# Seventy-five more products on cleared operands at the head of TensorE's program

## The reference

```python
x = x + 0.5 * post1(SwiGLU_1(pre1(x)))
u = pre_mix(x);  [MLA inputs | MoBA q,k,v] = u @ W_in
y = W_out(concat[RMSNorm(MLA heads), RMSNorm(MoBA heads)])
x = x + post_mix(y)
x = x + 0.5 * post2(SwiGLU_2(pre2(x)))
```

## Time and profile before

| | us |
|---|---|
| median of 2 runs | 1759.57 |
| the two runs | 1759.31, 1759.82 |
| span of the profiled execution, first to last instruction | 1756.5 |
| TensorE busy in it | 1737.1 (99%) |
| first product of the real work starts at | 8.89 |

### The profile page before, as it was taken

One profiled execution on the slowest core, in us unless ns is written; L12 is line 12 of the kernel. 1 busy time (PEld: TensorE's weight loads), 2 busy tenths in 40 slices (PEclk: granted clock), 3 DMA queues, 4 the chain that ended last, 5 costly groups with the idle time before them and its releaser, 6 DMA issues. The chain is left out here.

```text
span 1756.5 us, 21394 instructions
## 1 busy us (share of the span) xinstructions
PE 1737.1 (99%) x7968; PEld 1442.3 (82%) x7968; DVE 1410.7 (80%) x1284; ACT 1001.8 (57%) x979; POOL 65.3 (4%) x99
## 2 busy tenths in 40 slices
PE   9999999999999999999999999999999999999998
PEld 8788888888888888788888878788888888888886
DVE  7888888888888888765578558888888888888887
ACT  6666565555655654543347446555666666555563
POOL 1000000000000000010000000000000000000000
PEclk9999999999999999999999999999999999999999
DMA  9777777777766554355441546777777777666453
GB/s 386 237 257 259 256 256 239 239 239 248 245 234 222 184 215 176 147 219 189 174 162 54 187 171 260 263 240 241 249 249 241 239 246 251 254 232 238 174 191 114
DMA packets 58978, 389.75 MB, mean 222 GB/s; under 512 B 6432, under 2 KB 6688, under 8 KB 16160
## 3 DMA queue, kind: packets, MB, share of 16 engines
q1 hardware_dynamic: 52720, 344.77, 50.1%
q0 software_dynamic: 6048, 44.04, 13.2%
q10 hardware_dynamic: 144, 0.04, 0.0%
HBM read 384.63 MB, written 4.19 MB: 221 GB/s over the span
## 5 line engine op out<-in xcount | busy, mean ns | idle before, releaser
L2093 PE MATMUL banks<-w_hi,act_hi 128*128 128x512 f32 (+1 forms) x1088 | 424.7, 390 | 1.1 <-DVE act_lo L1355 1.1
L2095 PE MATMUL banks<-w_hi,act_lo 128*128 128x512 f32 (+1 forms) x1088 | 421.5, 387 | 0.0
L2094 PE MATMUL banks<-w_lo,act_hi 128*128 128x512 f32 (+1 forms) x1088 | 421.2, 387 | 0.0
L1385 DVE TENSOR_TENSOR op_lo<-quads,op_hi 128x2048 fp32r<-128x2048 f32 x140 | 318.5, 2288 | 43.2 <-ACT op_hi L918 42.8
L918 ACT ACTIVATE op_hi<-quads 128x2048 fp32r<-128x2048 f32 x140 | 266.8, 1919 | 53.3 <-PE banks L2095 21.1
L2287 PE MATMUL banks<-w_hi,hid_split 128*128 128x512 f32 x992 | 275.1, 389 | 0.5 <-DVE hid_split L1616 0.5
L1374 DVE TENSOR_TENSOR w_lo<-raw,w_hi 128x2048 fp32r<-128x2048 f32 x80 | 181.3, 2287 | 78.3 <-ACT w_hi L892 78.3
L1344 DVE TENSOR_TENSOR w_lo<-raw,w_hi 128x2048 fp32r<-128x2048 f32 (+3 forms) x67 | 143.8, 2147 | 121.6 <-ACT w_hi L843 121.6
L2093 PEld LDWEIGHTS banks<-w_hi,act_hi 128*128 128x128 f32 x1088 | 204.6, 188 | 42.1 <-issue 1.8
L2095 PEld LDWEIGHTS banks<-w_hi,act_lo 128*128 128x128 f32 x1088 | 204.4, 188 | 41.7
L2094 PEld LDWEIGHTS banks<-w_lo,act_hi 128*128 128x128 f32 x1088 | 204.6, 188 | 40.0
(11 more groups left out here) (209 smaller groups left out, 2329.8 us busy)
## 6 DMA issues: line engine op xcount, KB each, us to landing
raw<-in_weights SPq DMA_DIRECT2D x203, 1024.0 KB, 5.1
quads<-in_paired SPq DMA_DIRECT2D x80, 1024.0 KB, 10.7
quads<-in_paired POOLq DMA_DIRECT2D x40, 1024.0 KB, 8.5
raw<-in_paired SPq DMA_DIRECT2D x32, 768.0 KB, 5.9
rows<-in_x SPq DMA_DIRECT2D x4, 1024.0 KB, 10.9
raw<-in_weights SPq DMA_DIRECT2D x6, 512.0 KB, 3.5
gain_row<-in_post_gains SPq DMA_DIRECT2D x3, 1024.0 KB, 6.6
raw<-in_weights SPq DMA_DIRECT2D x4, 768.0 KB, 4.1
```

The lines of the kernel that those rows point to most:

```text
L1385: nc.vector.tensor_tensor(op_lo[:, slot, :], op_raw(op), op_hi[slot][:, :], ALU.subtract)\
L2093: nc.tensor.matmul(out_ap, hi, rhs_hi, start=start, stop=False, skip_group_check=chain)
L2094: nc.tensor.matmul(out_ap, hi, rhs_lo, start=False, stop=False, skip_group_check=chain)
L2095: return nc.tensor.matmul(out_ap, lo, rhs_hi, start=False, stop=stop, skip_group_check=chain)
```

## The change

GpSimd clears the whole of `op_split` (3072 columns of four bytes) right behind `mask` and ahead of `ident`, and raises `field_cleared`. TensorE waits for it behind the 20 warm products and then issues 75 products into bank 5, all with start and stop set, before it waits for `consts_made` and goes on as before. Fourteen shapes of five products each use `op_split` as F32R: `(lhs, rhs, cols, width)` gives the shift of the stationary operand from column 2816, the first column of the streamed operand, the number of stationary columns, and the number of streamed columns. Twelve of them stream 512 columns from 128 stationary ones, one has 96 stationary columns, and one streams 256. The last five products read the same bytes as BF16.

```diff
+WARM_EACH = 5
+WARM_SHAPES = ((0, 0, 128, 512), (2, 0, 128, 512), (4, 0, 128, 512), (16, 0, 128, 512), (64, 0, 128, 512),
+               (0, 2, 128, 512), (0, 4, 128, 512), (0, 16, 128, 512), (0, 64, 128, 512), (0, 128, 128, 512),
+               (0, 0, 96, 512), (0, 0, 128, 256), (-2560, 0, 128, 512), (0, 0, 128, 512))
...
+        field_cleared = sem("field_cleared")
...
             nc.gpsimd.memset(mask[:, :], 0.0).then_inc(mask_cleared, 1)
+            nc.gpsimd.memset(op_split[:, :, :].bitcast(F32), 0.0).then_inc(field_cleared, 1)
             nc.gpsimd.memset(ident[:, :], 0.0)
...
+            def warm_on_cleared_operands():
+
+                field = op_split[:, :, :].rearrange("p k n -> p (k n)")
+                half = field.bitcast(BF16)
+                far = 2 * D_OPERAND - 2 * P
+                for lhs, rhs, cols, width in WARM_SHAPES:
+                    for _ in range(WARM_EACH):
+                        nc.tensor.matmul(banks[0:cols, 5, 0:width], field[:, far + lhs:far + lhs + cols],
+                                         field[:, rhs:rhs + width], start=True, stop=True)
+                for _ in range(WARM_EACH):
+                    nc.tensor.matmul(banks[:, 5, :], half[:, 2 * far:2 * far + P], half[:, 0:BANK], start=True, stop=True)
+
             pe.wait_ge(mask_cleared, 1)
             for _ in range(WARM):
                 nc.tensor.matmul(banks[:, 5, 0:P], mask[:, 0:P], mask[:, 0:P], start=True, stop=True)
+            pe.wait_ge(field_cleared, 1)
+            warm_on_cleared_operands()
             pe.wait_ge(consts_made, 1)
             gate_up(GU1, 0)
```

## The result

| | before | after |
|---|---|---|
| median of 2 runs, us | 1759.57 | 1773.27 (1772.90, 1773.64) |
| span of the profiled execution | 1756.5 | 1771.2 |
| its own time | not given | 1772.9 |
| second real product starts at | 9.19 | 24.42 |

The ratio is 1.0079, 95% interval 1.0061 to 1.0097. The change makes the kernel 13.7 us slower; the forecast was 15.1 us slower, 1774.7. Timed again in five runs it came out the same: 1771.97 against 1758.64 for the kernel before on the same chip, 13.3 us, ratio 1.0079 (1.0065 to 1.0092).

The account below looks back on a forecast made before the run. TensorE's stream of products was taken as the bound: real work starts 15.37 us later, less 0.25 given back, so 15.1 on a span of 1756.5 makes 1771.6, plus 3.07 gives 1774.7 us; range 1770.5 to 1781.

Parts of the forecast that it names:

- What bounds the kernel: Whole span: TensorE's own stream of products sets the end, busy 1737.1 of 1756.5 us, 0.2267 us a product.
- The clock at the head: Warm products: the clock rises to 2.4 GHz inside them, so more warm products have nothing left to speed up.
- The clearing, the wait, the later constants: Head: GpSimd's clearing takes 2.7 us, covered by 20 warm products; later constants cost 0, the wait counts in the stream's start.
- The 75 products: TensorE's head: 14.74 us for 65 F32R, 0.59 for five of 256 columns, 1.13 for five BF16; together 16.46 us.
- Given back: Early real work: two gaps of 0.13 us each go as operands are ready early; 0.25 us given back.
- the two gaps that I named: TensorE just behind its operands from 8.89 to 12.19 us, and a late `act_lo` for piece 2 at 19.67; 0.13 us each.
- the stalls of the earlier trace: Far on, between VectorE and TensorE: claimed that a shifted start does not touch them, so nothing is given back there.
- From span to median: Final sum: the median before stands 3.07 us over its span, so a span of 1771.6 gives 1774.7 us.
- shorter products in the body: Rival, 7968 matrix instructions of the body: 1.9 ns less each would pay the 15.1 us; chance 0.03.
- Shifted groups: Rival, 50 new products with shifted operands: at twice the pace they take 11.3 us more, 1786.0; chance 0.08.
- F32R is one instruction: Answers a rival: F32R operands treated as plain F32, 0.89 us per 512 columns, 44.7 us more, 1819.4; chance 0.02.
- The delay is not hidden: Answers a rival: the late start replaces later TensorE stalls; if 8.6 us of them went, 1766.1; chance 0.03.

Follow-up runs that it names:

- the second 75: The changed kernel with ten products per shape instead of five, 150 in all: 29.5 us over the kernel before, ratio 1.0173; the added products cost 16.2 us.
- the plain F32 kernel: The changed kernel with 18 products of 512 columns read as plain F32 in place of the 75: 14.0 us over the kernel before, ratio 1.0073.

## Why the prediction was right, point by point

- **What bounds the kernel.** Right. A delay at the head of TensorE's stream arrives at the end nearly whole: 15.2 us at the second real product, 14.7 in the span, 13.7 and 13.3 in the medians; 16.2 for the second 75.
- **The clock at the head.** Right. The rise came inside the warm products, at 4.9 us after and at 5.5 before, so more warm products had nothing to speed up. The earlier rise moved the last warm product from 7.71 to 7.43 us, and the stream began at 7.5 us and not at 7.8 for this reason.
- **The clearing, the wait, the later constants: 0.** Right, 1.0002 with these alone.
- **The 75 products: 16.46 us.** Measured 16.6. By the records the stream runs from 7.46 to 24.00, but where the type changes the first record starts early (0.315 us to the next at 7.46, 0.42 at 24.00, where the pace is 0.227); with the pace behind each it runs from 7.55 to 24.19. The terms: 0.227 for an unshifted product as forecast, 0.232 in the shifted groups where I had 0.227, 0.118 for 256 columns as extrapolated, and 0.216 for BF16 where I had 0.227 ((1.03 - 0.38) / 3 in the row above, with 0.38 us for one record, is 0.217). The errors of about +0.2 and -0.06 are nothing here. On BF16 the rule of the Trainium skill, page "TensorE: Matmul & The Clock Gate", section "Back-to-back issue gap", the columns over 2.4 GHz and 2.5 ns more, which is 215.8 ns for 512, agrees with the measured 216; the F32R products of these runs, at 226.7 ns and more, do not keep it.
- **Given back: 0.25 us.** This is the term that was mis-sized: measured 1.35 us in one trace and 1.57 in the other. Of the two gaps that I named, the one at piece 2 gave back its 0.13 us (the lag falls from 15.20 to 15.07 there), the one behind the first product only 0.03. The step that failed is the sentence that the stalls of the earlier trace rows are not touched by a shifted start. Two of them went, 0.5 us at `part` and 0.7 at `hid`, with the slow starts around them. The reason is one that I had not looked at: not the time added, but the number of instructions, by which a block of them was fetched elsewhere.
- **From span to median: +3.07.** Right as it was used, though I had its meaning wrong. It is not what lies before the first instruction and behind the last: that is 1.6 to 1.8 us. The rest is that the profiled execution before was likely some 1.4 us shorter than the median of its two neighbours. Added to the profiled span it gives the median before again, and so the forecast is that median plus 15.1 us. The median moved by 13.7, and the 1.4 us between them are about what the two stalls gave back, 1.2 us, and the 0.14 at the start. An offset of 1.7 would have given 1773.3, nearer by luck alone: it would have put a short execution before against a median after.
- **The rivals.** No shorter products in the body: the pace stays at 227 ns (0.2268 in the rows of the study). Shifted groups are slower, but by 5 ns and not 227. F32R is one instruction. The delay is not hidden.
- **What stays open.** Counted product by product against the trace of the kernel before, the lag stays at 13.9 us from 92 to 132 us, is 14.5 up to 174 and 14.2 from there to 711, rises to 15.1, falls to 14.4 at 1047 to 1049, goes between 13.5 and 15.1 from 1126 to 1217, and stays at 14.7 to the end. One dip of the granted clock sits at 725 us after (711 in the time of the kernel before) and at 1046 before, which accounts for the steps of 0.9 and 0.8 us at these two places. The other steps, at 132, at 174 and from 1126 to 1217 us, were not taken apart. And in the plain F32 kernel the same piece came late (71.0 us) with its block of instructions at 60.2. There the packets of GpSimd's accumulating transfer ended at 69.5 us; in the other kernels they ended between 66.9 and 69.0. So a fetch in the wrong place is one cause of that late piece and not the only one.

## What to carry to other kernels

Where one engine's stream sets the end, put what you add against what it was waiting for: up to the arrival of its first operands it is free, and from there on each product costs its pace, to a few per cent. Before giving an added instruction the price of its time alone, ask where the blocks of instructions behind it are now fetched; in a stretch where the DMA engines are full, this took away or brought back 1 us of stalls. For a difference below 1%, compare medians with medians: one profiled execution can lie 1.4 us beside the median of its own kernel.

## What the runs showed of the hardware

- A 16 KB packet of instructions took 0.93 us of a busy DMA engine here. 150 more instructions on TensorE brought it 15 us earlier in the work, 256 put it back to its place (67.7 against 67.9 us).
- F32R products of 512 columns whose operand is shifted by 1 to 32 columns started 230 to 236 ns apart in the mean of a group. Unshifted and at 64 columns they settled at 227, at once or after some five products; one unshifted group of ten stayed at 232. 96 or 64 stationary columns were not faster (230).
- Products of 32 by 32 columns start 31.5 ns apart, BF16 of 512 columns 216 ns, plain F32 of 512 columns 859 ns (two instructions).
- TensorE stood still from 8.1 to 26.6 us; its granted clock was 0.50 at the end of that, and seven products, 0.43 us apart, passed before it was 1.00 again.
